# A transformer block on one core: first top-k cut into four parts beside the query projections, later top-ks respread over the dots, tails in another order beside the last rows

## The reference, cut to what matters

```python
x = x + (mg[:, :, 0] * y_a + mg[:, :, 1] * y_b) @ w_o          # mixers (before the change's place)
x = x + peer(rmsnorm(x, g_ffn), peer_wq, peer_k1, peer_k2, peer_u, peer_v)
x = x + jax.nn.sigmoid(rmsnorm(x, g_ple) @ w_ple_gate) * (p @ w_ple)
out = rmsnorm(x, g_final)

def peer(h, w_q, sub_k1, sub_k2, u, v):
    q = (h @ w_q).reshape(B, S, 8, 2, 128)
    s1, s2 = q[..., 0, :] @ sub_k1.T, q[..., 1, :] @ sub_k2.T   # 128 keys each
    v1, i1 = top_k(s1, 16);  v2, i2 = top_k(s2, 16)
    cand, cidx = v1[..., :, None] + v2[..., None, :], i1[..., :, None] * 128 + i2[..., None, :]
    sc, pos = top_k(cand, 16)                                   # 16 experts of 16384, for each of 8 heads
    eidx, gate = cidx[pos], softmax(sc)
    act = gelu(einsum('td,thkd->thk', h, u[eidx]))
    return einsum('thk,thkd->td', gate * act, v[eidx])
```

## Time and profile before

| | |
|---|---|
| median of 3 runs | 1987.89 us (1982.43 to 1994.17) |
| the profiled execution | 1976.98 us, span of its instructions 1975.2 us |
| PE, PE weight load, DVE, ACT, POOL busy | 1749.3, 1115.3, 1135.4, 244.5, 697.2 us |
| moved by DMA | 475.53 MB, 241 GB/s over the span |
| granted TensorE clock, mean over the span | 0.931 of full |
| chain that ended last | PE 53%, DMA 27%, DVE 13%, POOL 4% |

### The profile page before, as it was taken

One profiled execution on the slowest core, in us unless ns is written; L12 is line 12 of the kernel. 1 busy time (PEld: TensorE's weight loads), 2 busy tenths in 40 slices (PEclk: granted clock), 3 DMA queues, 4 the chain that ended last, 5 costly groups with the idle time before them and its releaser, 6 DMA issues.

```text
span 1975.2 us, 17251 instructions
## 1 busy us (share of the span) xinstructions
PE 1749.3 (89%) x6170; PEld 1115.3 (56%) x6170; DVE 1135.4 (57%) x2433; ACT 244.5 (12%) x601; POOL 697.2 (35%) x714
## 2 busy tenths in 40 slices
PE   6979899999999899999999993777999999999067
PEld 3454344343678488888888883666444444443033
DVE  0011233232120999999984558999666555567933
ACT  2002232223110102111111110000000000000023
POOL 0001233333000223343343446777645333445700
PEclk9979999999999999999999997666999999999589
DMA  6231110000544579999998998333999999999911
GB/s 200 75 117 54 32 33 22 22 11 0 178 131 152 189 262 348 370 359 380 354 374 328 409 409 345 107 107 107 383 409 409 409 409 409 409 409 408 409 48 43
DMA packets 131969, 475.53 MB, mean 241 GB/s; under 512 B 14715, under 2 KB 15739, under 8 KB 131884
## 3 DMA queue, kind: packets, MB, share of 16 engines
q0 software_dynamic: 73728, 268.47, 35.4%
q1 hardware_dynamic: 58156, 205.97, 28.1%
HBM read 471.19 MB, written 3.19 MB: 240 GB/s over the span
## 4 chain that ended last, share of the span: by engine, by line
PE 53%; DMA 27%; DVE 13%; POOL 4%; issue 2%; ACT 1%; SPq 0%; DVEq 0%; ACTq 0%; POOLq 0%
DMA arena<-in_v,eidx 20%; PE psum L1366 16%; PE psum L1215 6%; DMA arena<-in_u,eidx 6%; PE psum L1277 6%; PE psum L1113 5%; POOL arena L477 3%; PE psum L1193 3%; PE psum L1326 3%; PE psum L1237 3%; PE psum L1249 3%; PE psum L1165 2%; DVE arena L951 2%; DVE arena L1006 2%; DVE arena L1009 2%
## 5 line engine op out<-in xcount | busy, mean ns | idle before, releaser
L1366 PE MATMUL psum<-arena 128*128 128x256 f32 x2048 | 442.5, 379 | 0.7 <-ACT arena L589 0.7
L1384 PE MATMUL psum<-arena 128*128 128x512 f32 x1024 | 440.4, 593 | 2.1 <-DMA arena<-in_vd 1.4
L477 POOL DMA_INDIRECT arena<-in_u,eidx x256 | 247.2, 965 | 517.2 <-DVE dots L951 292.3
L973 DVE SCALAR_TENSOR_TENSOR arena<-arena,wts 128x1024 f32<-128x1024 f32 x254 | 325.5, 1285 | 172.7 <-DMA arena<-in_v,eidx 172.6
L1366 PEld LDWEIGHTS psum<-arena 128*128 128x128 f32 x2048 | 389.3, 190 | 53.4 <-ACT arena L589 0.9
L477 POOL DMA_INDIRECT arena<-in_v,eidx x256 | 252.7, 987 | 250.0 <-DVE arena L973 223.0
L951 DVE CUSTOM_DVE_ANT_0 arena<-psum,arena 128x1024 f32<-128x1024 f32 x256 | 304.4, 1221 | 59.8 <-DMA arena<-in_u,eidx 57.8
L1384 PEld LDWEIGHTS psum<-arena 128*128 128x128 f32 x1024 | 194.4, 190 | 246.8 <-issue 242.8
L458 POOL TENSOR_SCALAR arena<-arena 128x256 f32<-128x256 f32 (+4 forms) x128 | 105.9, 846 | 376.5 <-DVE arena L747 245.0
L1377 PE MATMUL psum<-arena 128*128 128x128 f32 x512 | 111.2, 387 | 74.6 <-POOL arena L487 29.4
L1377 PEld LDWEIGHTS psum<-arena 128*128 128x128 f32 x512 | 97.2, 284 | 88.9 <-DVE arena L1009 54.4
(11 more groups left out here) (167 smaller groups left out, 1351.2 us busy)
## 6 DMA issues: line engine op xcount, KB each, us to landing
arena<-in_ut SPq DMA_DIRECT2D x128, 512.0 KB, 6.8
arena<-in_vd SPq DMA_DIRECT2D x128, 512.0 KB, 6.8
arena<-in_wpack SPq DMA_DIRECT2D x105, 512.0 KB, 3.6
arena<-in_u,eidx POOLq DMA_INDIRECT x256, 9.2
arena<-in_v,eidx POOLq DMA_INDIRECT x256, 14.7
arena<-in_w_pg SPq DMA_DIRECT2D x8, 512.0 KB, 9.0
arena<-in_x SPq DMA_DIRECT2D x4, 512.0 KB, 4.9
arena<-bias_rows SPq DMA_DIRECT2D x8, 256.0 KB, 5.6
```

Source lines behind the costliest of these rows:

```text
L477: G.indirect_dma_start(out=slots[n % SLOTS], out_offset=None, in_=a["v"] if values else a["u"], in_offset=bass.IndirectOffsetOnAxis(ap=eid ...
L973: V.scalar_tensor_tensor(to, row, w, to, ALU.mult, ALU.add).then_inc(row_used, 1)
L1366: last = T.matmul(ps[6 + c % 2][:, 0:DT], u[:, k * P:(k + 1) * P], h2T1[:, k, :], start=(k == 0), stop=(k == KC - 1))
L1384: last = T.matmul(ps[BANK + 2 * t + h], mixed[:, c, t * P:(t + 1) * P], stream[:, c % SRING, h * HALF:(h + 1) * HALF], start=(c == 0), sto ...
```

## The change

Four things are moved; the arithmetic is the same.

1. PE's order around the first top-k: up(1) stops after two chunks; queries(0) follows, with the four parts of scores(0) put between its projections; then the other six chunks of up(1) and project_out(1). The weight blocks go in this order too (`B_UP1B`). DVE starts each quarter of tile 0's top-k when its part is there, and the merges 2 to 7 of the second half stand between the steps of that top-k. Merges 4 and 5, and one head with its `publish`, come before the last two merges.
2. The later top-ks: all `top_of_halves` within the first 27 dots, the rest from columns 34, 72 and 106 (own `vals` and `idxu` for tiles 2 and 3); `gates` at 30, 84, 120 and, for tile 3, at 20 of tile 1; `gate_exp` after blocks 48, 68 and 92. `W_AT` falls from 96 to 72.
3. From gather 464 on (`accumulate(1, 80)`) only 6 slots are used, and tiles 2 and 3 of `xs` are fetched back then.
4. Tails in the order 0, 2, 3, 1 (`TAIL_ORDER`), with the DVE work of the first three put between the last 24 rows of tile 1. `tail_turn(3)` comes after `tail_embed(2)`; ACT's `tail_norm(3)` after `tail_last_norm(2)`. `sum_out` is split into `rows_summed` and `dense_added`.

```diff
-B_WQ0 = B_UP1 + KC
-B_WO1 = B_WQ0 + 2 * PH
+B_WQ0 = B_UP1 + 2
+B_UP1B = B_WQ0 + 2 * PH
+B_WO1 = B_UP1B + KC - 2
...
-W_AT = 96
+W_AT = 72
+LAST_ROWS = 464
...
+        def slot_of(n):
+            return n % SLOTS if n < LAST_ROWS else (n - LAST_ROWS) % 6
+
+        def gathered(n):
+            s = slot_of(n)
+            return row_gathered[s], 16 * (n // SLOTS + 1 if n < LAST_ROWS else LAST_ROWS // SLOTS + (n - LAST_ROWS) // 6 + 1)
+
+        def slot_free(n):
+            if n < LAST_ROWS:
+                return n - SLOTS + 1
+            return n - 6 + 1 if n - LAST_ROWS >= 6 else n - SLOTS + 1
+
 
...
+            sp.wait_ge(row_used, LAST_ROWS)
             for t in range(NG, TILES):
                 sp.dma_start(xs[:, t, :], xdram[t - NG, :, :]).then_inc(rows_back, 16)
...
-                if c == 24:
+                if c == 48:
                     gate_exp(1)
-                if c == 56:
+                if c == 68:
                     gate_exp(2)
-                if c == 88:
+                if c == 92:
                     gate_exp(3)
...
             tail_gate(1)
-            tail_norm(3)
             tail_last_norm(1)
             tail_gate(2)
             tail_last_norm(2)
+            tail_norm(3)
             tail_gate(3)
             tail_last_norm(3)
...
-            for m in range(1, KC):
-                merge(1, m)
+            merge(1, 1)
 
...
             for c in range(4):
                 top_of_halves(0, 4 * c, 4 * c + 4)
-            pair_up()
+            pair_up(0)
+            merge(1, 2)
+            merge(1, 3)
             top_pairs(0)
+            merge(1, 4)
+            merge(1, 5)
+            number_experts(0, 0, 1)
+            publish(0, 0, 1)
+            merge(1, 6)
+            merge(1, 7)
+            number_experts(0, 1, 4)
             add_mixer(2)
             add_mixer(3)
-            number_experts(0, 0, 1)
-            publish(0, 0, 1)
-            number_experts(0, 1, 2)
+            number_experts(0, 4, 5)
...
+                for t in range(1, TILES):
+                    h = 2 + 8 * (t - 1)
+                    if k in (h, h + 4):
+                        top_of_halves(t, 2 * (k - h), 2 * (k - h) + 8)
+                for t, base in ((1, 34), (2, 72), (3, 106)):
+                    i = k - base
+                    if i == 0:
+                        pair_up(t)
+                    if i == 4:
+                        top_pairs(t)
+                    if i in (8, 12, 16, 20):
+                        number_experts(t, (i - 8) // 2, (i - 8) // 2 + 2)
+                    if i == 21:
+                        if t < NG:
+                            publish(t, 0, PH)
+                        else:
+                            split(t)
...
             for k in range(COLS):
                 dot(0, k)
-                for t in range(1, TILES):
-                    later_top(t, k - 2 - 42 * (t - 1))
-                if k == 20:
+                later_top(k)
+                if k == 30:
                     gates(0)
-                if k == 62:
+                if k == 84:
                     gates(1)
-                if k == 104:
+                if k == 120:
                     gates(2)
             dve.wait_ge(row_used, COLS)
             V.tensor_copy(hp2, hn[1]).then_inc(dot_rows_ready, 1)
             dve.wait_ge(dot_rows_ready, 2)
             for k in range(W_AT):
                 dot(1, k)
-                if k == 10:
+                if k == 20:
                     gates(3)
...
-            for k in range(COLS):
-                accumulate(1, k)
-                if k == 8:
-                    tail_scale(0)
-            close(1)
-            dve.wait_ge(rows_back, 16 * (TILES - NG))
...
+            def rows(k0, k1):
+                for k in range(k0, k1):
+                    accumulate(1, k)
+
+            rows(0, 104)
+            tail_scale(0)
+            dve.wait_ge(rows_back, 16 * (TILES - NG))
             add_dense(2)
             tail_turned(0)
+            rows(104, 106)
             add_dense(3)
+            rows(106, 108)
             tail_scale(1)
+            rows(108, 110)
             tail_turned(1)
+            rows(110, 114)
             tail_add(0)
+            rows(114, 116)
             tail_scale(2)
             tail_turned(2)
             tail_out(0)
+            rows(116, 120)
             tail_add(1)
+            rows(120, 124)
+            tail_out(1)
+            rows(124, 128)
+            close(1)
+            tail_add(2)
             tail_scale(3)
             tail_turned(3)
-            tail_out(1)
-            tail_add(2)
             tail_out(2)
             tail_add(3)
...
-            up(0)
+            for m in range(KC):
+                up(0, m)
             project_out(0)
-            up(1)
+            up(1, 0)
+            up(1, 1)
             turn(0)
-            queries(0, h2T0)
-            scores(0)
+            for p in range(PH):
+                queries(0, p)
+                if p >= 3 and p % 2:
+                    key_scores(0, p // 2 - 1)
+            key_scores(0, 3)
+            pe.wait_ge(query_out, PH)
+            for m in range(2, KC):
+                up(1, m)
             pe.wait_ge(keyscores_out, 4)
             project_out(1)
-            pe.wait_ge(query_out, PH)
-            scores(1)
...
+            for p in range(PH):
+                queries(1, p)
             pe.wait_ge(query_out, 2 * PH)
-            scores(2)
-            scores(3)
+            for t in range(NG, TILES):
+                for c in range(4):
+                    key_scores(t, c)
             pe.wait_ge(keyscores_out, 4 * TILES)
...
                 values(c, 1).then_inc(values_made, 1)
-            for t in range(TILES):
-                tail_gate(t)
-                if t + 1 < TILES:
-                    tail_turn(t + 1)
-                tail_embed(t)
+            for p in range(TILES):
+                tail_gate(p)
+                if p < 2:
+                    tail_turn(p + 1)
+                tail_embed(p)
+                if p == 2:
+                    tail_turn(3)
```

287 lines of the change are left out of this document (152 added, 135 removed).

## The result

The changed kernel took **2011.38 us** (median of five runs, 1998.65 to 2046.66) against 1982.43 us of the kernel before (five runs, 1980.89 to 1994.17). The ratio, formed without the run of 2046.66, is 1.0106 (95% interval 1.0058 to 1.0154): **slower by 1.1%, about 21 us**. The forecast was 1978, 10 faster, with a range up to 1993.

The account below looks back on a forecast made before the run. Bounds: PE in projections, dense scores and tails; DVE's dots before the mix and the mix; DMA in the rows. Against 1975.2, -18.8 - 1 + 2.6 + 7.2 gave 1965.3; shifted to the runs' median, 1978, range 1962 to 1993.

Parts of the forecast that it names:

- the dense scores, ended at 1195.2 + 5.0 = 1200.2, now end last: Before the mix: 72 dots done at 1177, so the mix begins at 1200.2 instead of 1219.0, -18.8 us.
- The sum, without holes: Whole kernel: all terms together give 1965.3 us against the profiled 1975.2, about 10 faster.
- forecast +5.0: Projections: a new PE hole of 9 us replaces the old; queries(1) begins at 692.8 instead of 687.84.
- the 2.0 for a restart: project_out(1) after PE's new 9 us hole: 2.0 us added for PE restarting after idling.
- I count it at full clock: Transposes ahead of queries(1): after a hole of only 2.9 us they take 2.6 us, with no half-clock loss.
- DVE waits 13 us at 916 and 24 at 1057: Dots: DVE waits for ACT's Exps after blocks 48 and 92, which come at 929 and 1081.
- -18.8 - 1 at the mix: Mix: begins 18.8 us earlier and takes 1 us less, since PE comes to it without a long wait.
- T + 98.4: Tails: from row 103 of tile 1 done (T, 1866.9) to the span's end, 98.4 us.
- +7.2 from row 103 on: Tails: 98.4 us from accumulate(1, 103) on, where 91.2 us had followed row 127.
- a better start: Projections: PE's new hole is filled and the norms keep their old time; 1971 us, 22%.
- PE's clock stays low: project_out(1): half clock throughout costs 27.7 us more instead of 2.0; 2004 us, 10%.
- The rows stretch: Last rows: six slots or interleaved waits cost 6 to 8 us more; 1986 us, no measurable change, 20%.

Follow-up runs that it names:

- the first two jobs: Sets of runs on one chip: changed kernel, its parts alone, then the dots' common row in SBUF; kernel before had medians of 2052.07 and 2043.59 us.
- the run without holes: Changed kernel unaltered, profiled in a later set of runs, PE without idle gaps in the dense scores: 1971.66 us; that set's median 1968.95 against 1977.70 for the kernel before.
- the one of 2020.58 us: Changed kernel unaltered, profiled on a chip with PE idle gaps in the dense scores; median there 2028.23 us, kernel before 2052.07.
- the padded dots: Changed kernel plus a small DVE copy ahead of each dot, dots' common row in PSUM: 1976.33 us, later 1980.80.
- the five gathers of the third job: Changed kernel with at most five gathers under way instead of eight up to dot 200: 1978.55 us, kernel before 1977.98.
- the fifth job: Changed kernel with only `W_AT` back from 72 to 96: 1963.71 us, ratio 0.9933 to the kernel before.
- C alone: Kernel before plus only the tails' part (`W_AT` 72, six slots, new tail order): 2028.52 us; with the dots' common row moved to SBUF, 1966.28.
- the row in SBUF: `hp2`, the row every dot multiplies, moved from PSUM to SBUF: changed kernel 1977.74 us, kernel before 1989.17, tails' part only 1966.28.
- half dots from SBUF: Changed kernel with dots over 512 of 1024 columns and `hp2` in SBUF: 1959.93, 1959.27 and 1961.48 us in three sets of runs.

## Why the prediction was wrong, step by step

*The step that failed* is the sentence "the dense scores, ended at 1195.2 + 5.0 = 1200.2, now end last", and in it the unspoken premise that PE goes through this stage at 3.46 us a block whatever DVE and the gathers do. The row behind it (PE busy 132.60 of 132.70 us) was one execution of a kernel that, on the chip of the first two jobs, takes 2040 to 2061 us in 18 of 29 runs and 1980 to 2008 in the others. The forecast had a rival with half the clock, none in which PE's signals come late. What the runs showed in its place: in the result's own profile the dense scores take 77.9 us more than in the run without holes, in the one of 2020.58 us 48.5, and neither loses anything elsewhere. That the result's other four runs lost their time there too is read from these profiles, since they have none of their own.

*The sum, without holes*, gave 9.9 us; measured 8.8 (1977.70 to 1968.95). That is closer than its parts were, and in part luck.

- Projections, forecast +5.0: from the begin of up(0) to that of the dense scores it is 262.8 us (498.0 to 760.8) instead of 256.4 (495.7 to 752.1), **+6.4**. project_out(1) took 29.12, as the 2.0 for a restart had it nearly (27.7 + 1.4), and queries(1) 58.0 instead of 55.5, a term that I had at nothing: after a hole of 2.96 us PE runs its first queries at half pace (6.21 us for 16 matmuls, where 64 take 13.98), at a granted clock of 0.59 from 693.9 to 700.2. "I count it at full clock" was wrong by 2.5 here, but not always. Of the 15 profiled executions with these projections, all with the same hole, 9 have the 58.0, among them all three of the changed kernel; 6 have 55.5 at a clock of 1.00 (the padded dots and the five gathers of the third job, for example), and there the stage costs 3.7 to 4.2 instead of 6.4. The 5.0 lies between the two.
- Dots. Forecast: DVE waits 13 us at 916 and 24 at 1057 for the Exps. Neither came without holes. The Exps ran when forecast (930.69 and 1082.64 for 929 and 1081), but DVE arrived at 946.5 and 1085.2, after them. The missed step is a wait that stood in the diff: quarters of tile 2's top-k now begin at column 10, near 734, and need its key scores, which PE makes only after queries(1):

```profile
755.39 1.65 DVE L857 MAX8 arena<-arena 128x8 f32<-128x128 f32 x8 [21.55 <-ACT arena L613]
```

  While DVE waits, the slots are full and DMA idles: from 700 to 800 its share is 0.66, where it was 0.87. The rest of the way the dots run behind the gathers. So the forecast had two waits that did not come and missed one that did. It cost nothing, since 72 dots were done at 1191.1 instead of 1177, still 12.78 us ahead of the dense scores' end instead of 23: the 23 us to spare covered the error, not the reasoning. In the run of 2020.58 us, where the gathers race ahead of PE, DVE does wait for an Exp, 46.8 us at the longest.

- Mix. Forecast 1200.2 to 1361.9; 1203.8 to 1365.2, right as a length (161.4 for 161.7).
- 24 dots after it, forecast 502.4 + 2.6 to row 103; 506.7. Right. The reading that the earlier mix is what gains ("-18.8 - 1 at the mix") was bookkeeping: the fifth job shows that this pair of terms is a wash.
- Tails, forecast T + 98.4; **T + 98.0**. Its steps: first gate T + 2.7 (2.7), DVE waits for PE until T + 19.4 (19.8) and T + 37.4 (37.9), last gate T + 69.1 (68.3). The rows of these steps, DVE's two waits and PE's last gate:

```profile
1891.76 1.29 DVE L951 TENSOR_TENSOR arena<-psum,small 128x512 f32<-128x512 f32 x2 [8.88 <-PE psum L1388]
1909.81 1.29 DVE L951 TENSOR_TENSOR arena<-psum,small 128x512 f32<-128x512 f32 x2 [7.04 <-PE psum L1388]
1940.21 16.31 PE L1397 MATMUL psum<-arena 128*128 128x512 f32 x32 [7.12 <-DVE arena L951]
```

  Before, row 103 was done at 1884.1 - 24 x 1.28 = 1853.4 and the rest took 121.8. **The tails' order is worth 24 us and is the whole gain**: C alone against the kernel before, both with the row in SBUF, is 1966.28 to 1989.17, -22.9. C holds the six slots and the early fetch of tiles 2 and 3 as well, which were not run apart; the third view of C's expectation, that these cost 0 to 10 us, falls. The forecast's +7.2 from row 103 on, and its sentence "the tail's overlap hides little more than the 24 dots that were pushed behind the mix", set these 24 us against the time of the 24 dots, which the fifth job measured as 32 and which the earlier mix had already won back.
- The table load that spoke against a Sqrt between two Sigmoids took 1.28 us again, as the earlier trace rows had it; the sum with 1.4 more would have been 99.8 and farther off.
- Rivals: "a better start" did not come (the hole was 8.34 us). "PE's clock stays low" did not come either; project_out(1) lost 1.4 us, not 27.7. "The rows stretch" did not come: 506.7 against the 505.0 of the forecast.

**What stays open.** Why PE's done signal is late. Shown: in the long holes the gathers take all of the DMA time; the signal is late with DVE reading PSUM 54% of the time (0.69 in 1.28 us) or 95% (1.22 in 1.28); in C's holes the stream's blocks and ACT are not what it waits for; with the dots' row in SBUF no run of 28 was long on the chip where others were. Not shown: whether that is so because PSUM is no longer read, or because the gathers' issue got slower than DMA. The half dots from SBUF and the padded dots would have told, and never ran where holes show. Nor is it known what sets one chip apart from another (no run tells the chip from the time of the job), or why in the result the changed kernel shows the loss and the kernel before, at 1981 to 1994 in five runs, does not.

## What to carry to other kernels

Read from a profile who waits for whom in a hole down to the signal: a stream that moves little may be a stream that nobody asks for. When a change moves work from one side of a stage to the other, sum both sides before calling either a gain; here 25 to 27 us won ahead of the mix were 32 paid behind it, and the gain was made by overlap in the tail alone. A forecast made from one execution of a kernel whose stage is full on two engines and on DMA needs a case for the stage's other state, and its test needs the kernel before on the same chip.

## What the runs showed of the hardware

- A second state of a stage in which the engines that wait for PE's completion signal see it 9 to 45 us after the last matmul's start, while engines and DMA queues beside it go on at full pace (DMA 410 GB/s, DVE 18.13 of 19.00 us). On one chip the kernel before has the times that go with it in 18 of 29 runs, on three others in none of 42.
- An indirect DMA's issue on POOL took 955 ns beside dots with one operand in PSUM, and 1358 ns beside dots with both in SBUF; beside half dots from SBUF 1063 to 1074 in three executions.
- The gathers alone moved 409 to 410 GB/s into SBUF in a hole, as much as gathers and stream together outside of one.
- After the same 2.96 us or so without matmuls PE took 58.0 us for queries(1) in 9 executions (in the one without holes 6.21 us for the first 16 matmuls, at a granted clock of 0.59, where full pace is 3.5) and 55.5 us in 6, at 1.00.
